# Router product on four column strips, prompt rows of the experts gathered as half rows

## What is computed

```python
x = _layer_norm(DEEPNORM_ALPHA * x + mix, ln1_g, ln1_b)
x = _layer_norm(DEEPNORM_ALPHA * x + _expert_choice_ffn(x, ...), ln2_g, ln2_b)

def _expert_choice_ffn(x, w_router, w_gate, w_up, w_down):
    cap = max(1, (CAPACITY_FACTOR * t) // N_EXPERTS)      # 128 for the sample, 64 for the prompt
    aff = jax.nn.softmax(jnp.einsum('td,de->te', xt, w_router), axis=-1)
    gate, idx = lax.top_k(aff.T, cap)
    xe = xt[idx]
    h = jax.nn.silu(jnp.einsum('ecd,edf->ecf', xe, w_gate)) * jnp.einsum('ecd,edf->ecf', xe, w_up)
    ye = jnp.einsum('ecf,efd->ecd', h, w_down) * gate[..., None]
    return zeros.at[idx.reshape(-1)].add(ye.reshape(-1, d))
```

## Time and profile before

| | us |
|---|---|
| Median of 3 runs (1345.35 to 1348.69) | 1347.62 |
| The profiled execution, its own time | 1353.78 |
| Span of the profiled execution, first to last instruction | 1352.0 |
| TensorE busy in the span | 1200.3 (89%) |
| VectorE busy | 920.6 (68%) |
| ScalarE busy | 686.6 (51%) |
| GpSimd busy | 363.4 (27%) |
| Mix, from about 594 to 834 | 240 |
| Experts and last norm, from 834 to 1352 | 518 |

### The profile page before, as it was taken

One profiled execution on the slowest core, in us unless ns is written; L12 is line 12 of the kernel. 1 busy time (PEld: TensorE's weight loads), 2 busy tenths in 40 slices (PEclk: granted clock), 3 DMA queues, 4 the chain that ended last, 5 costly groups with the idle time before them and its releaser, 6 DMA issues. The chain is left out here.

```text
span 1352.0 us, 21821 instructions
## 1 busy us (share of the span) xinstructions
PE 1200.3 (89%) x7374; PEld 1076.7 (80%) x7374; DVE 920.6 (68%) x1536; ACT 686.6 (51%) x1191; POOL 363.4 (27%) x434
## 2 busy tenths in 40 slices
PE   4999997798999999969999962999999999999960
PEld 4999986687888888857878742999999999999960
DVE  7755523587878778756446784777777777777738
ACT  4222222465666676642222231666667666666636
POOL 1322200356410000001221114233334433333317
PEclk9999997898999999979999975999999999999985
DMA  8255446932311011048455443798888889888738
GB/s 296 100 168 168 150 154 229 293 98 78 106 39 48 8 31 32 13 136 260 148 165 161 161 182 117 229 267 280 272 264 266 272 264 276 284 266 254 217 79 336
DMA packets 161220, 242.24 MB, mean 179 GB/s; under 512 B 13233, under 2 KB 123409, under 8 KB 161169
## 3 DMA queue, kind: packets, MB, share of 16 engines
q1 hardware_dynamic: 151312, 206.97, 46.4%
q0 software_dynamic: 9856, 34.61, 9.7%
HBM read 179.37 MB, written 62.18 MB: 179 GB/s over the span
## 5 line engine op out<-in xcount | busy, mean ns | idle before, releaser
L2166 PE MATMUL ps_gate_up<-xT_hi_lo,w_hi 128*128 128x384 f32 x896 | 263.9, 358 | 1.4 <-DVE xT_hi_lo L2091 1.4
L2167 PE MATMUL ps_gate_up<-xT_hi_lo,w_lo 128*128 128x192 f32 x896 | 225.6, 252 | 0.0
L2086 DVE TENSOR_TENSOR w_lo<-w_raw,w_hi 128x2048 fp32r<-128x2048 f32 x93 | 212.2, 2282 | 0.0
L2026 ACT ACTIVATE w_hi<-w_raw 128x2048 fp32r<-128x2048 f32 x92 | 175.8, 1911 | 0.0
L2167 PEld LDWEIGHTS ps_gate_up<-xT_hi_lo,w_lo 128*128 128x128 f32 x896 | 172.2, 192 | 0.6
L2166 PEld LDWEIGHTS ps_gate_up<-xT_hi_lo,w_hi 128*128 128x128 f32 x896 | 170.2, 190 | 2.4 <-issue 1.7
L979 DVE TENSOR_REDUCE neg_max<-ps_scores 128x1 f32<-128x1024 f32 (+1 forms) x80 | 97.6, 1220 | 44.2 <-PE ps_scores L76 43.6
L873 ACT ACTIVATE pT_hi<-ps_probsT 128x512 fp32r<-128x512 f32 x160 | 87.1, 596 | 75.8 <-PE ps_probsT L1107 75.3
L1942 POOL TENSOR_TENSOR d_wait_carrier<-d_zero 128x1 f32<-128x1 f32 x78 | 33.3, 427 | 292.1 <-PE ps_xT L2155 151.8
L991 DVE TENSOR_TENSOR pT_lo<-ps_probsT,pT_hi 128x512 fp32r<-128x512 f32 x160 | 101.5, 674 | 4.2 <-ACT pT_hi L873 4.2
L882 ACT ACTIVATE probs<-ps_scores,neg_max 128x1024 f32<-128x1024 f32 (+1 forms) x96 | 93.5, 978 | 16.1 <-DVE neg_max L979 15.9
(11 more groups left out here) (273 smaller groups left out, 3180.7 us busy)
## 6 DMA issues: line engine op xcount, KB each, us to landing
w_raw<-in_w_gate SPq DMA_DIRECT2D x32, 1024.0 KB, 8.9
w_raw<-in_w_up SPq DMA_DIRECT2D x32, 1024.0 KB, 8.5
w_raw<-in_w_down SPq DMA_DIRECT2D x32, 1024.0 KB, 7.1
scratch_x<-x SPq DMA_DIRECT2D x24, 512.0 KB, 2.7
scratch_v<-v_out SPq DMA_DIRECT2D x12, 512.0 KB, 5.3
v_hi_lo<-scratch_v SPq DMA_DIRECT2D x8, 768.0 KB, 4.9
x_again<-scratch_x SPq DMA_DIRECT2D x12, 512.0 KB, 3.7
scratch_acc<-acc_out SPq DMA_DIRECT2D x12, 512.0 KB, 3.1
```

The source lines that it names most:

```text
L2026: act.activation(w_hi[c][:, :], raw[:, c, :], ACT.Copy).then_inc(hi_done, 1)
L2086: nc.vector.tensor_tensor(w_lo[c][:, :], raw[:, c, :], f32(w_hi[c][:, :]), ALU.subtract).then_inc(lo_done, 1)
L2166: nc.tensor.matmul(ps[:, 0:2 * N], w_hi[chunk][:, at], xT[:, k, :], start=k == 0, stop=False)
L2167: nc.tensor.matmul(ps[:, 0:N], w_lo[chunk][:, at], xT[:, k, 0:N], start=False, stop=False)
```

## The change

It puts two edits into one kernel.

*Router product.* `w_router` becomes 32 columns wide for each block (16 experts, 16 zeros, filled by GpSimd). The eight matmuls no longer add up in the same 16 rows: block k goes to column strip k mod 4 of the array and to 32 rows of the PSUM bank of its own, so that each strip adds up two blocks. ScalarE copies all 128 rows to `logitsT`. In place of the transpose a product with `add_groups` (128 x 16, ones where row and expert belong together) turns the logits and adds the four strips at once. GpSimd makes `add_groups` from `ident` at the start of the mix. SP waits for the fill before it loads `w_router`.

*Prompt rows.* The 64 prompt rows of an expert are gathered as 128 half rows of 2 KB: partitions 0 to 63 hold channels 0 to 511, partitions 64 to 127 channels 512 to 1023 of the same tokens. VectorE makes their indices in `route_prompt_halves` (twice the token, plus one in the lower half). Pairs are now blocks p and p+4, and one transpose turns the prompt columns of both. The zero fill of `x_rows_prompt` goes away.

```diff
-        w_router = m.sb("w_router", [P, KD, N_EXPERTS])
-        logitsT, ... = m.sb("logitsT", [N_EXPERTS, P]), ...
+        GROUPS, STRIP = 4, 32
+        w_router, add_groups = m.sb("w_router", [P, KD, STRIP]), m.sb("add_groups", [P, N_EXPERTS])
+        logitsT, ... = m.sb("logitsT", [P, P]), ...
...
-            sp.dma_start(w_router[:, :, :], dram["w_router"].rearrange("(k p) e -> p k e", p=P)).then_inc(ln_loaded, 16)
+            sp.wait_ge(filled, 7)
+            sp.dma_start(w_router[:, :, 0:N_EXPERTS], dram["w_router"].rearrange("(k p) e -> p k e", p=P)).then_inc(ln_loaded, 16)
...
-            pool.memset(first_rows.prompt[:, :], 0.0).then_inc(first_rows.zeroed, 1)
...
-            pool.wait_ge(filled, 6)
+            pool.memset(w_router[:, :, :], 0.0).then_inc(filled, 1)
+            pool.wait_ge(filled, 7)
+            strips = ident[:, :].rearrange("p (g c) -> p c g", g=GROUPS)[:, 0:N_EXPERTS, :]
+            pool.tensor_tensor(add_groups[:, :], strips[:, :, 0], strips[:, :, 1], ALU.add).then_inc(groups_step, 1)
+            for g in range(2, GROUPS):
+                pool.wait_ge(groups_step, g - 1)
+                pool.tensor_tensor(add_groups[:, :], add_groups[:, :], strips[:, :, g], ALU.add).then_inc(groups_step, 1)
...
-            pool.wait_ge(lists_copied, 2)
-            for q, rows in enumerate(first_rows.into):
-                pool.indirect_dma_start(rows, None, dram["x1"], ...)
+            for q, (rows, source) in enumerate(zip(first_rows.into, first_rows.sources(dram))):
+                pool.wait_ge(lists_copied, q + 2)
+                pool.indirect_dma_start(rows, None, source, ...)
...
-                    act.activation(logitsT[:, :], ps_r[0:N_EXPERTS, 0:P], ACT.Copy).then_inc(logits_copied, 1)
+                    act.activation(logitsT[:, :], ps_r[:, 0:P], ACT.Copy).then_inc(logits_copied, 1)
...
+            nc.vector.tensor_reduce(second_half[:, :], ident[:, CAP_PROMPT:2 * CAP_PROMPT], op=ALU.add, axis=AX.X).then_inc(half_known, 1)
             scale_attention(0, 0)
...
             nc.vector.tensor_copy(route["tokens"][:, :, :], token_f[:, :, :]).then_inc(lists_copied, 1)
+            dve.wait_ge(half_known, 1)
+            nc.vector.tensor_scalar(route["rows"][1], token_f[:, 1, :], 2.0, second_half[:, 0:1], ALU.mult, ALU.add).then_inc(lists_copied, 1)
...
                     for k in range(KD):
-                        last = nc.tensor.matmul(ps_r[0:N_EXPERTS, 0:P], w_router[:, k, :], x1T[:, k, :], start=k == 0, stop=k == KD - 1)
+                        g = k % GROUPS
+                        last = nc.tensor.matmul(ps_r[g * STRIP:(g + 1) * STRIP, 0:P], w_router[:, k, :], x1T[:, k, :],
+                                                start=k < GROUPS, stop=k >= KD - GROUPS, tile_position=(0, g * STRIP))
...
-                    nc.tensor.transpose(ps_a[:, 0:N_EXPERTS], logitsT[:, :], ident[0:N_EXPERTS, 0:N_EXPERTS]).then_inc(logits_turned, 1)
+                    nc.tensor.matmul(ps_a[:, 0:N_EXPERTS], logitsT[:, :], add_groups[:, :], start=True, stop=True).then_inc(logits_turned, 1)
...
+    def sources(self, dram):
+        return dram["x1"], dram["x1"].rearrange("t (h c) -> (t h) c", h=2)
...
-                act.activation(xT[:, 2 * pair:2 * pair + 2, 0:N],
+                act.activation(xT[:, pair:pair + 5:4, 0:N],
                                ps_turn[pair][:, :, 0:N], ACT.Copy).then_inc(x_hi_done, 1)
...
-                for k in range(2):
-                    src = slice((2 * pair + k) * P, (2 * pair + k + 1) * P)
-                    nc.tensor.transpose(ps_turn[pair][:, k, 0:P], x_rows[:, src], ident[:, :])
-                    last = nc.tensor.transpose(ps_turn[pair][:, k, P:2 * P], x_rows_p[:, src], ident[:, :])
-                last.then_inc(x_turned, 1)
+                for x, k in enumerate((pair, pair + 4)):
+                    nc.tensor.transpose(ps_turn[pair][:, x, 0:P], x_rows[:, k * P:(k + 1) * P], ident[:, :])
+                nc.tensor.transpose(ps_turn[pair][:, :, P:P + CP], x_rows_p[:, pair * P:(pair + 1) * P], ident[:, :]).then_inc(x_turned, 1)
```

More of the change, by code:

```diff
@@ L1407, in _ @@
                 pool.wait_ge(x1_stored[s], 16 * N_TILES // 2)
-            pool.wait_ge(lists_copied, 2)
-            for q, rows in enumerate(first_rows.into):
-                pool.indirect_dma_start(rows, None, dram["x1"],
-                                        bass.IndirectOffsetOnAxis(ap=route["token"][q][0:rows.shape[0], 0:1], axis=0)).then_inc(first_rows.gathered[q], 16)
+            for q, (rows, source) in enumerate(zip(first_rows.into, first_rows.sources(dram))):
+                pool.wait_ge(lists_copied, q + 2)
+                pool.indirect_dma_start(rows, None, source,
+                                        bass.IndirectOffsetOnAxis(ap=route["rows"][q][:, 0:1], axis=0)).then_inc(first_rows.gathered[q], 16)
         @block.scalar
@@ L1492, in _ @@
             dve.wait_ge(ln_loaded, 48)
-            dve.wait_ge(filled, 6)
+            dve.wait_ge(filled, 7)
             now, buffer, n_steps = affT, 0, 0
@@ L1682, in step @@
                     pe.wait_ge(ln_loaded, 48)
+                    pe.wait_ge(groups_step, GROUPS - 1)
                 if has(s, 1):
@@ L1709, in __init__ @@
     def __init__(self, m):
-        self.sample, self.prompt = m.sb("x_rows_sample", [CAP_SAMPLE, D]), m.sb("x_rows_prompt", [P, D])
-        self.into = (self.sample[:, :], self.prompt[0:CAP_PROMPT, :])
+        self.sample, self.prompt = m.sb("x_rows_sample", [CAP_SAMPLE, D]), m.sb("x_rows_prompt_halves", [P, D // 2])
+        self.into = (self.sample[:, :], self.prompt[:, :])
         self.gathered = [m.sem(f"rows_gathered{q}") for q in range(2)]
-        self.zeroed = m.sem("rows_zeroed")
+    def sources(self, dram):
+        return dram["x1"], dram["x1"].rearrange("t (h c) -> (t h) c", h=2)
 class OutputNorm:
@@ L1945, in copy_index, with gather @@
                 for q in range(2):
[L1946 to L1951, removed]
+                    pool.tensor_copy(gather_at[q][:, :], route["rows"][q][:, bass.ds(e, 1)]).then_inc(index_copied, 1)
+            def gather(q):
+                pool.indirect_dma_start(first_rows.into[q], None, first_rows.sources(dram)[q],
+                                        bass.IndirectOffsetOnAxis(ap=gather_at[q][:, 0:1], axis=0)).then_inc(gathered[q], 16)
             def scatter_add(q, rows):
@@ L1972, in gather_rows @@
                 pool_carrier()
-                gather(0, x_rows)
-                gather(1, x_rows_p[0:CP, :])
+                gather(0)
+                gather(1)
             def copy_lists(e, carriers):
@@ L2089, in rest_x @@
                 dve.wait_ge(x_hi_done, 4 * e + pair + 1)
-                hi = f32(xT[:, 2 * pair:2 * pair + 2, 0:N])
-                nc.vector.tensor_tensor(xT[:, 2 * pair:2 * pair + 2, N:2 * N],
+                hi = f32(xT[:, pair:pair + 5:4, 0:N])
+                nc.vector.tensor_tensor(xT[:, pair:pair + 5:4, N:2 * N],
                                         ps_turn[pair][:, :, 0:N], hi,
@@ L2284, in build @@
         tokens, gates = m.sb("route_token", [P, 2, N_EXPERTS], U32), m.sb("route_gate", [P, 2, N_EXPERTS])
-        route = {"tokens": tokens, "gates": gates,
+        halves = m.sb("route_prompt_halves", [P, N_EXPERTS], U32)
+        route = {"tokens": tokens, "gates": gates, "rows": [tokens[:, 0, :], halves[:, :]],
                  "token": [tokens[:, q, :] for q in range(2)], "gate": [gates[:, q, :] for q in range(2)]}
```

9 lines of the change are left out of this document (4 added, 5 removed).

## The result

| | us |
|---|---|
| Before, median of 4 runs (1345.35 to 1348.69) | 1348.07 |
| After, median of 4 runs (1328.96 to 1329.59) | 1329.33 |
| Ratio after to before, 95% interval | 0.9864 [0.985, 0.9878] |
| The profiled execution of after, its span | 1329.58, 1327.8 |

The changed kernel is faster by 18.7 us, or 1.4%. The sum said 11.6 us. Most of the difference sits in the mix: 11.5 us where the sum had 4.3.

The account below looks back on a forecast made before the run. TensorE's issue was taken to bound mix steps 2 to 9 and the experts' loop. Gains of 4.7 (mix), 6.6 (loop) and 0.34 us (expert 0) summed to 11.6, taking the median from 1347.62 to 1336.0 us, range 1331 to 1344.5.

Parts of the forecast that it names:

- The sum: Whole kernel: 4.7 us from the mix, 6.6 from the loop and 0.34 at expert 0, 11.6 us gained.
- What bounds the kernel: Mix steps 2 to 9 and experts' loop: TensorE's issue sets the pace; from step 10 VectorE leads.
- The router product: Mix, each tile: sixteen passes on strips, two at a time, take 1.20 us in place of 1.85, saving 0.65.
- The rival with four strips at once: Router product takes 0.62 us, 1.12 us net a tile, 16.3 us in all, 1331.3 us; chance 0.22.
- order rule: Router product: passes start in order, so the next block's first pass starts only with this block's second.
- The product with `add_groups`: Mix, turning of the logits: two passes in place of the transpose cost 0.11 us more, ends 0 and 0.27.
- How many tiles pay: Mix: the eight of steps 2 to 9 pay 0.54 us each, 4.3 us; step 11 at most 0.38.
- the wrong term: Mix, router product with turned logits: net saving of 0.54 us a tile.
- The 0.38 us of step 11: Mix, step 11: the router product can gain no more than TensorE's release lets VectorE save, its wait of 0.38 us.
- The loop: Experts 1 to 15: four transposes fewer each, at a slot of 0.11 us, gain 6.6 us; nothing else binds.
- Expert 0: Start of the experts: three transposes fewer at 0.21 us gain 0.64 us, less the gather's charge, net 0.34 us.
- The charge against it: Expert 0, gather of half rows: 0.15 us more issue and 0.15 us later landing, with ends 0 and 0.9 for the landing.

Follow-up runs that it names:

- neighbours: The changed kernel with two neighbouring blocks of the router product on each strip (0 and 1 on strip 0, and so on), in place of 0 and 4; one run, 1328.14 us.
- router_only: The router edit alone (column strips and the product with `add_groups`), on the kernel before; 1335.87 us, ratio 0.9912.
- rows_only: The half-row edit alone (prompt rows gathered as half rows, one transpose for both blocks), on the kernel before; 1340.82 us, ratio 0.9939.

## Why the prediction was wrong, point by point

**What bounds the kernel** was right. TensorE's issue set the pace in both stages, before and after, and nothing that the sum called covered came to bind.

**The router product** is where the forecast failed, and at one step: "passes start in order, so the first pass of the next block can start only with the second of this one. Two run at a time". The term was 1.20 us; the runs show 0.58. The rival with four strips at once had 0.62, and its four slots hold. That the next work waits until the last pass has run out does not: by that working one strip would take 15 x 0.116 + 0.273 = 2.01 us and two 1.09, where 1.86 and 1.00 were measured. I gave this rival 0.22 because two passes of a block are neighbours on the same strip, and `neighbours`, with four on a strip in a row, shows that this hardly matters (0.02 us). The trace of before could not decide it, since it has no two strips; I gave 0.54 to an order rule that no row showed. The Trainium skill (TensorEngine Tiling (Array Packing), Theoretical Speedup) states up to four times for operands of at most 32 columns; measured are 1.85 / 0.58 = 3.2 times, slots for four and a piece at the end. Another rule of the Trainium skill, that weight loads overlap matmuls in flight only where the row group differs (TensorE: Matmul & The Clock Gate, Part 3: Packing small matmuls — row/col tiling), does not hold here: loads of 110 ns for four column strips, which share all rows, stay hidden, 16 of them in 0.58 us. The same section of the Trainium skill says that matmuls start and end strictly in program order; `neighbours` shows that this does not hold a free strip back.

**The product with `add_groups`** had the wrong sign. I charged 0.11 us with the ends 0 and 0.27, and took no gain into the bounds, although nothing excluded one: I counted passes and did not ask what the 16 rows of the old transpose cost around it. The row that shows it stood in the trace of before, just ahead of the two that I had read the earlier trace rows. TensorE in order of time, before:

```profile
709.04 0.39 PE L76 MATMUL ps_mix<-w_hi,mix_lo 128*128 128x512 f32 x1
...
709.87 0.40 PE L75 MATMUL ps_mix<-w_lo,mix_hi 128*128 128x512 f32 x1
```

The transpose started at 709.36, 0.32 us after the first of these, where products of full height start 0.23 apart; the second, two matmuls behind the transpose, started 0.34 us after the one ahead of it. Measured -0.15 us in place of +0.11. Over eight tiles this is 8 x 0.26 = 2.1 us, and it is what puts the time outside the range: four strips at once came to 1331.3 with +0.11, and with -0.15 it would have been 1329.2.

**How many tiles pay** was right: eight. After them the wait for the affinities in step 10 grew from 1.30 to 1.82 us. That this is the forecast number (about 1.8) is luck: it was 1.30 plus the 0.54 us of the wrong term, and with the 1.44 us that a tile really saved the same working gives 2.7. What came is 0.75 us of waiting for `mix_lo` and 1.82 for the affinities, 2.57 together. The 0.38 us of step 11 came as well, as far as one profiled execution each can tell: from the ninth router product to expert 0 it took 70.95 us before and 70.57 in `router_only`. In the changed kernel's own profile it is 70.75, for another reason, told in the last section.

**The loop** was right: 0.45 us an expert, 15 x 0.45 = 6.75 us against 6.6, with TensorE busy in 425.00 of 425.00 us. The gather did not press: by the tile's view it holds GpSimd for 1.96 us a time (median; 1.90 before) and lands at most 8.9 us after issue (9.7 before).

**Expert 0** had the right gain, 0.64 us, to the hundredth in `rows_only` and after (5.59 to 4.95). The charge against it was wrong: I took off 0.30 us for the gather, and the way from the first gather to the barrier became 0.37 us shorter (6.40 to 6.03; over all profiles 6.21 to 6.40 in the three with whole rows, 5.84 to 6.05 in the seven with half rows). Here too the bounds, 0 and 0.9, left out a gain. The reason that I gave, twice the packets, finds no support either. The page's list of DMA queues counts as many packets and MB on GpSimd's queue as before (9856, 34.61):

```profile
q0 software_dynamic: 9856, 34.61, 9.8%
```

Why the half rows land earlier was not explored.

**The sum from the runs**: 11.5 (steps 2 to 9) + 0.4 (step 11) + 6.75 (loop) + 0.64 + 0.37 (expert 0) = 19.7 us, against 18.7 measured, with an interval of 16.4 to 20.2. One stretch is not in this sum: from the mix's first matmul to the router product of step 2 the two profiles have 36.9 us before and 37.9 after. In step 1 TensorE waits for `mix_lo`, and VectorE, which makes it, waits for the landing of `w_router`, 3.05 us before and 3.52 after:

```profile
622.07 0.69 DVE L1472 TENSOR_TENSOR mix_lo<-mix_raw,mix_hi 128x512 fp32r<-128x512 f32 x1 [3.05 <-DMA w_router<-in_w_router]
```
```profile
618.54 0.69 DVE L1480 TENSOR_TENSOR mix_lo<-mix_raw,mix_hi 128x512 fp32r<-128x512 f32 x1 [3.52 <-DMA w_router<-in_w_router]
```

So the load of `w_router` lies on the path in both kernels. SP's wait for the fill ahead of it, which I costed at nothing, is not what delays it: SP issues the load right behind the one ahead of it (609.36; that one ends at 609.32). Over the profiles the stretch is 36.9 to 37.3 us in the three without the router edit and 37.0 to 37.9 in the seven with it; whether the edit costs some tenths there stays open.

In the profiles the stage from expert 0 on gained 9.0 us (517.6 to 508.6), 1.6 more than the loop and the turning give. 1.33 of these are the clock at the experts' start: TensorE worked 6.14 us at the lower clock from the first gate product on before, and 3.48 after. This stretch ran from 3.9 to 6.1 us in the four kernels with four transposes a pair and from 3.3 to 4.8 in the six with three, so most of it is scatter. Over all ten the stage lasts 516.5 to 517.6 us with four and 508.6 to 509.7 with three, 7.7 between the means, where loop and turning give 7.4.

**What stays open** is what makes a strip's slot of 0.11 us. The load (97 ns with 16 columns, 110 ns with 32) is close to it, but the slot was the same with either. Nor was it tried why a low stationary operand costs more around it, only that it does at 16, 32 and 64 rows.

## What to carry to other kernels

A chain of small products with few output columns can be dealt out over column strips, and the order of the passes hardly matters (13.85 or 13.90 us a step): count the passes of the fullest strip. Look at the distances around a matmul, to the one ahead and the one behind, and not only at its own slot: a low operand among full ones pays there, and filling it up with zeros can be cheaper. And where a price is not in the trace, let its bound go below zero unless a reason forbids it: both of my unknown charges (0.11 us for the logits, 0.30 us for the gather) turned out to be gains.

## What the runs showed of the hardware

The same waits do not always cost the clock. In the changed kernel's profile TensorE waited 0.75 and 1.82 us in step 10, and worked at the lower clock for the next 3 us; in `neighbours` it waited 0.71 and 1.82 us and kept the higher one. The windows right behind the wait, after first, then `neighbours`:

```profile
759.50:762.50 3.00, 2.93 (x8) 2.36 (x9) 2.70 (x6) 0.52 (x2) 0.02 (x1) 0.50 1.09 355
```
```profile
758.40:761.40 3.00, 2.91 (x13) 2.44 (x14) 2.73 (x6) 0.55 (x2) 0.00 (x0) 1.00 1.08 357
```

Eight matmuls at a granted clock of 0.50 (1.2 of 2.4 GHz) against thirteen at 1.00. It cost the step 1.5 us (18.33 against 16.83 from router product to router product), of which all but 0.5 to 0.6 was hidden, VectorE's chain being the longer one there: 70.75 us from the ninth router product to expert 0, against 70.14 to 70.30 in four other kernels with both edits on several strips. The lag is there by the last router product, 36.45 us after the ninth in place of 35.91 in `neighbours`. Without the second kernel I would have put the missing gain of step 11 down to the change.
